# A two-layer trunk: attention scores in three f32r products, an earlier start of the second projection, the dense stage's loads in another order, and the mLSTM cell's state update and squares moved

## The chip, the cores and the metric

The kernel runs on one core of a Trainium2 chip. Its time is device microseconds (us) of one execution on that core. Engines are called by their names in the profile: PE is TensorE's matmuls, PEld its weight loads, DVE is VectorE, ACT is ScalarE, POOL is GpSimd and SP is SyncE, which here only issues DMAs. "SPq" and "ACTq" are these engines' queues of issued DMAs and waits. Each engine works through its own instructions in order; semaphores tie them together.

## The reference, cut to what matters

Two layers on a sequence of 2048 positions of width 1024. Layer 0 runs an S5 recurrence and an mLSTM cell side by side; layer 1 is sliding-window attention. All in fp32.

```
h = x
# layer 0
proj = rmsnorm_mod(h) @ ev_w_in;  s5_u, s5_z, m_in, m_z = split(proj)
y_s5 = s5(s5_u) * silu(s5_z)                      # chunked scan, then a gated product with w_glu
xc = silu(conv(m_in)); q, k = xc @ wq, xc @ wk; v, o = m_in @ wv, sigmoid(m_in @ wo)   # per head, 4 heads of 256
for each chunk of 128 positions, each head:       # the mLSTM cell
    s = (q k^T) * exp(gates);  num = s v + g * q C;  den = sum(s) + g * q n
    C = decay * C + (w_k * k)^T v;  n = decay * n + sum(w_k * k)
    h_cell = num / max(|den|, exp(-m))
y_m = (rmsnorm(o * h_cell) * norm_g + skip * xc) * silu(m_z)
h = h + gate0 * (concat(y_s5, y_m) @ ev_w_out)
# layer 1
q, k, v, z = split(rmsnorm_mod(h) @ od_w_in);  q, k = rope(rmsnorm(q)), rope(rmsnorm(k))
for each block of 128 queries, window of 256 keys, 16 heads of 64, 4 key heads:
    p = softmax(masked(q k^T / 8), with a sink);  a = p v
h = h + gate1 * ((a * silu(z)) @ od_w_out)
```

## The kernel before

The program is a row of stages with a barrier between them: `startup`, `front` (first half of the first projection), `project2` (second half of it, with the S5 recurrence beside it), `glu`, `dense`, `cell`, `attend_in`, `attend`. Large products are made from values split into an f32r part and its f32r rest: ScalarE rounds (a CAST), VectorE subtracts, and TensorE adds three products (high by high, high by rest, rest by high), each of 128x128 weights and 512 columns.

**`project2` (L914).** For 64 groups g, `state(g)` makes two products of the group's matrices (L1207, L1208, out of a ring of buffers `s_wt` that SyncE fills), `gemm(s)` is a unit of 24 matmuls of the projection, and `y(g)` the group's output. TensorE's order is `state(s)`, `gemm(s)`, `y(s−1)`.

**`dense` (L1555).** 16 units u: for head u // 4 and 512 positions, the products for q and k (from `x`, i.e. `xc`, the first 12 matmuls) and for v and o (from `m`), and beside them the output product of the S5 half. `unit(u)` is on SyncE the load of both inputs (L1617, L1618 into `bridge`), on ScalarE their rounding (L1720, L1723), on VectorE the rests (L1786). `head(h)` loads and splits a head's weights into `e_wh`. `result(u, j)` on ScalarE takes one result out of PSUM and stores it. `gates` are the cell's gates, made from logits in small steps between the units; `Gates.transfers(sp, part)` (L1456) is SyncE's share: part 0 stores the logits, part 2 waits for VectorE's chunk ends and stores them (L1469).

**`cell` (L1916).** 16 chunks c of 128 positions, each with four heads h. Chunk c's instructions on each engine:
- TensorE, `first(c, h)`: transpose of the keys and scores (`xp_ks`, L2391, L2393), then queries by state (`xp_bb`, L2402). `second(c, h)`: keys by values (`xp_c`, C0 and C1, L2414, L2415), then scores by values (`xp_aa`, L2419). It goes `first(c, h+1)` before `second(c, h)`. The output product of the chunk before (`xp_o`, L2442 to L2444, 24 matmuls for each half n) and the transposes of `x_hs` (L2430) stand between the heads.
- ScalarE: `first(c, h)` scales keys (`x_kw`, L2092) and `BB` (`x_bs`, L2096); `square(c, h)` (L2100); `exps(c)` (L2080) makes the decays `x_pm` of chunk c, at the end of chunk c−1; `y_part` (L2123) rounds the output; `norm(c)` (L2135) squares the finished residual row of chunk c and sums it, for the next layer's norm.
- VectorE: `weigh(c, h)` (`x_st`, L2197) scores by decays; `state(c, h)` (L2203, L2204) adds C0 and C1 to the state `x_c`; `output(c, h)` (L2212 to L2222); `blend` (L2244, L2251); `residual(c, n)` (L2262) adds the output product to the residual.
- GpSimd: for each chunk one mask step (L2073) out of `gate_run`, input of `exps`.
- SyncE, in this order in each turn, all on one queue: `store(c−1)` (L2019), `residual(c)` (L2015), `xc(c+1)` (L2002), `inputs(c+2)` (keys L1988, queries L1989, `gate_run` L1992, values L1996, L1997), `z(c+1)` (L2007). This turn takes place while the engines work on chunk c+1.

The residual row has two buffers, so its load waits for the square of the chunk two before:

```python
def residual(c):
    if c >= 2:
        sp.wait_ge(h_out[c % 2], 16 * (c // 2))
        sp.wait_ge(h_squared, c - 1)
```

**`attend_in` (L2514).** 40 units of 24 matmuls: the projection into q, k, v, z. q and k are turned by VectorE (`rope`) into a ring `rst` of two, and SyncE stores each piece to `q_d`, `k_d`.

**`attend` (L3025).** 64 steps G (16 blocks t, 4 key heads g). In step G TensorE makes the products of weights by values of an earlier step (`b_pv`, L3251), the scores (`b_psc`, L3228) in fp32 on 64 rows, two heads side by side, the transposes of exponentials (`b_t`, L3238) and 12 matmuls of the output product (`b_po`, L3266 to L3268). The rest of a step goes over ScalarE (L3124), GpSimd (L3113) and VectorE (L3167).

## Time and profile before

| | |
|---|---|
| median of 3 runs | 2952.21 us (2948.35 to 2953.49) |
| the profiled execution | 2948.46 us, span 2946.6 us |
| PE busy | 2750.8 us, 93% of the span |
| PEld, DVE, ACT, POOL busy | 2184.4, 1584.6, 1099.7, 642.4 us |
| mean granted clock of TensorE | 0.969 |

By the first and last instructions of the stages: `project2` about 493 to 1042, `dense` 1210 to 1590, `cell` 1590 to 2047, `attend_in` 2047 to 2546, `attend` 2550 to 2946. A timeline gives the start of an instruction in us, its length, engine and line, the operation with its output and input, how many instructions the row stands for, and in brackets the idle time of the engine before it with what ended it. The waits are a table of engine and line, what ended the wait, us in total, number, longest.

### The profile page before, as it was taken

The page shows a single profiled execution, that of the slowest core. Times are in us where ns is not written, and L with a number is a line of the kernel's source. Part 1 is how long each engine was busy: PE and PEld are TensorE (multiplying, and loading weights), DVE is VectorE, ACT ScalarE, POOL GpSimd, SP SyncE. Part 2 cuts the span into 40 slices and gives each one's busy share as a digit, 9 for nine tenths or more (in the row PEclk, how much of TensorE's full clock was granted, in tenths as well). Part 3 has the DMA queues.
Part 4 walks back from the last instruction along what each step waited for, and adds up shares of the span by engine and source line. Part 5 has one row for each costly group of instructions (what it writes and reads, how often), then busy time and mean ns, then how long its engine had stood idle before and what let it go on. Part 6 is the DMA issues. An engine that isn't in the chain of part 4 may idle for free. (4 is left out here: it accounts for less than half of the span.)

```text
span 2946.6 us, 36815 instructions
## 1 busy us (share of the span) xinstructions
PE 2750.8 (93%) x13147; PEld 2184.4 (74%) x13147; DVE 1584.6 (54%) x3226; ACT 1099.7 (37%) x2380; POOL 642.4 (22%) x528
## 2 busy tenths in 40 slices
PE   4899998999999899799998799998999999899999
PEld 2787887888888678678886677776787777667776
DVE  5475771555665457454444666665533331466664
ACT  3612221222222223334432555554422221466664
POOL 0005651444545100022322000000000000133332
PEclk7999999999999899899998899998999999999999
DMA  8226446444554554788986565764322223522221
GB/s 278 88 70 149 152 152 146 142 148 143 147 154 149 164 202 165 256 252 247 292 269 203 146 171 163 211 166 136 99 70 80 77 84 117 164 65 86 87 92 60
DMA packets 461515, 445.07 MB, mean 151 GB/s; under 512 B 149685, under 2 KB 357901, under 8 KB 459917
## 3 DMA queue, kind: packets, MB, share of 16 engines
q1 hardware_dynamic: 357828, 337.20, 38.6%
q10 hardware_dynamic: 103504, 105.51, 10.7%
q8 instruction: 106, 1.74, 0.3%
q14 instruction: 77, 0.62, 0.1%
HBM read 280.98 MB, written 162.70 MB: 151 GB/s over the span
## 5 line engine op out<-in xcount | busy, mean ns | idle before, releaser
L2964 PE MATMUL a_pg<-a_hT,a_whl 128*128 128x512 f32 x640 | 256.8, 401 | 3.4 <-DVE a_whl L902 3.4
L2965 PE MATMUL a_pg<-a_hT,a_whl 128*128 128x512 f32 x640 | 251.2, 392 | 0.0
L2966 PE MATMUL a_pg<-a_hT,a_whl 128*128 128x512 f32 x640 | 250.9, 392 | 0.0
L908 PE MATMUL p_g<-hT,w_hl 128*128 128x512 f32 x512 | 212.3, 415 | 0.0
L854 PE MATMUL pg<-hT,w_hl 128*128 128x512 f32 x512 | 206.0, 402 | 6.4 <-DVE w_hl L902 6.4
L856 PE MATMUL pg<-hT,w_hl 128*128 128x512 f32 x512 | 201.5, 394 | 0.0
L855 PE MATMUL pg<-hT,w_hl 128*128 128x512 f32 x512 | 201.4, 393 | 0.0
L910 PE MATMUL p_g<-hT,w_hl 128*128 128x512 f32 x512 | 200.3, 391 | 0.0
L909 PE MATMUL p_g<-hT,w_hl 128*128 128x512 f32 x512 | 199.8, 390 | 0.0
L2964 PEld LDWEIGHTS a_pg<-a_hT,a_whl 128*128 128x128 f32 x640 | 121.4, 190 | 42.0 <-DVE a_whl L902 12.3
L2966 PEld LDWEIGHTS a_pg<-a_hT,a_whl 128*128 128x128 f32 x640 | 121.3, 190 | 26.3
L2965 PEld LDWEIGHTS a_pg<-a_hT,a_whl 128*128 128x128 f32 x640 | 121.6, 190 | 23.6
L1110 POOL TENSOR_TENSOR s_region<-s_wt 128x512 f32<-128x512 f32 x64 | 72.2, 1129 | 301.5 <-DMA s_wt<-s5w_d 301.3
L1130 DVE TENSOR_TENSOR s_region<-p_v,s_region 128x512 f32<-128x512 f32 x64 | 44.1, 690 | 166.0 <-PE p_v L1208 157.3
L3113 POOL TENSOR_TENSOR shared<-shared,b_stat 128x1024 f32<-128x1024 f32 x43 | 81.5, 1895 | 184.1 <-DVE b_stat L3180 184.1
L854 PEld LDWEIGHTS pg<-hT,w_hl 128*128 128x128 f32 x512 | 97.4, 190 | 29.4 <-DVE w_hl L902 7.3
L1395 PE MATMUL g_ps<-g_gh,g_w 128*128 128x512 f32 x256 | 101.5, 396 | 13.2 <-DVE g_gh L1297 10.0
L856 PEld LDWEIGHTS pg<-hT,w_hl 128*128 128x128 f32 x512 | 97.3, 190 | 21.0
L855 PEld LDWEIGHTS pg<-hT,w_hl 128*128 128x128 f32 x512 | 97.5, 190 | 19.1
L910 PEld LDWEIGHTS p_g<-hT,w_hl 128*128 128x128 f32 x512 | 96.2, 188 | 20.7
L909 PEld LDWEIGHTS p_g<-hT,w_hl 128*128 128x128 f32 x512 | 96.5, 188 | 20.0
L908 PEld LDWEIGHTS p_g<-hT,w_hl 128*128 128x128 f32 x512 | 96.6, 189 | 19.7
(546 smaller groups left out, 6854.2 us busy)
## 6 DMA issues: line engine op xcount, KB each, us to landing
s_wt<-s5w_d SPq DMA_DIRECT2D x64, 354.0 KB
w_raw<-in_ev_w_in SPq DMA_DIRECT2D x32, 512.0 KB, 6.1
s5w_d<-gate_sums SPq DMA_DIRECT2D x32, 512.0 KB, 3.1
vo_d<-e_stage ACTq DMA_DIRECT2D x64, 256.0 KB, 3.8
ada_w<-in_ada_w SPq DMA_DIRECT2D x32, 384.0 KB, 7.9
shared<-h_d SPq DMA_DIRECT2D x24, 512.0 KB, 3.9
a_raw<-in_od_w_in SPq DMA_DIRECT2D x38, 256.0 KB, 3.4
gate_sums<-h_d SPq DMA_DIRECT2D x18, 512.0 KB, 4.0
```

The lines of the kernel that those rows point to most:

```text
L854: nc.tensor.matmul(out, w[:, 0, k, :], x[:, 0, k, :], start=(k == 0), stop=False)
L855: nc.tensor.matmul(out, w[:, 0, k, :], x[:, 1, k, :], start=False, stop=False)
L856: last = nc.tensor.matmul(out, w[:, 1, k, :], x[:, 0, k, :], start=False, stop=(k == KC - 1))
L908: nc.tensor.matmul(out, w(0, k), x(0, k), start=(k == 0), stop=False)
L909: nc.tensor.matmul(out, w(0, k), x(1, k), start=False, stop=False)
L910: last = nc.tensor.matmul(out, w(1, k), x(0, k), start=False, stop=(k == n - 1))
L1110: table.add(nc.gpsimd.tensor_tensor(v4(pt), hi, lo(EBS), ALU.mult))
L1395: nc.tensor.matmul(ps[n][:], w(0), gh[:, 0, k, :], start=(k == 0), stop=False)
L2964: mm(bank, w[:, 0, k, :], x[:, 0, k, :], start=(k == 0), stop=False)
L2965: mm(bank, w[:, 0, k, :], x[:, 1, k, :], start=False, stop=False)
L2966: last = mm(bank, w[:, 1, k, :], x[:, 0, k, :], start=False, stop=(k == KC - 1))
L3113: nc.gpsimd.tensor_tensor(p, p, st[G % 3][:, 4].unsqueeze(2).broadcast_to([P, 4, 2 * P]), ALU.mult).then_inc(p_ready, 1)
```

## The change

- **`project2`**: in turn 0, TensorE does `gemm(0)` ahead of `state(0)`.
- **`dense`**: on SyncE the loads of unit 2 and of `y(1)` go ahead of the gates' first store and of the residual; heads 1 to 3 are loaded one unit later; `transfers(2)` goes from turn 2 to turn 3, behind unit 4's loads. On ScalarE and VectorE the rounding of `x` of unit 1 is separated from that of `m` and goes between results 4 and 5 of unit 0.
- **`cell`**: `state(c−1, 3)` goes ahead of `weigh(c, 0)` on VectorE, `blend(0)` ahead of a weight step; on ScalarE `norm(c−2)` at the end of turn c becomes `norm(c−3)` in the middle of it, behind `first(c, 2)`. SyncE's instructions are as they were.
- **`attend_in`**: each q piece is rounded (`q_round`) and its rest made (`q_rest`), and both are stored, to `q_d` and to a new `ql_d`; stores go out a unit later.
- **`attend`**: scores as three f32r products from `b_q_hi`, `b_q_lo`, `b_k_hi`, `b_k_lo`; the keys are split in five pieces, at the start and in steps 1, 9, 22, 38; the rests of the queries are loaded too. Some buffers get other places.

```diff
...
                 for s in range(LAST + 2):
-                    if s < LAST:
+                    if s == 0:
+                        gemm(0)
+                        state(0)
+                    elif s < LAST:
                         state(s)
                         gemm(s)
...
+        if part == "bias":
+            sp.dma_start(self.bias[:], self.a["m_b_if"].rearrange("o n -> n o"), allow_slow_non_contiguous=True).then_inc(self.bias_in, 16)
         if part == 0:
-            sp.dma_start(self.bias[:], self.a["m_b_if"].rearrange("o n -> n o"), allow_slow_non_contiguous=True).then_inc(self.bias_in, 16)
             sp.wait_ge(self.logits, 1)
             sp.dma_start(m.gt_d, m.gacc[:]).then_inc(self.moved, 16)
...
-                gates.transfers(sp, 0)
+                gates.transfers(sp, "bias")
                 for k in range(KC // 2, KC):
                     out_weight(k)
+                unit(2)
+                y(1)
                 sp.dma_start(gate[:], m.gate_d[0:1].broadcast_to([P, D])).then_inc(gate_in, 16)
                 x(0)
+                gates.transfers(sp, 0)
                 modulation(0)
                 for u in range(1, UNITS):
                     if u > 1:
                         modulation(u - 1)
-                    if u + 1 < UNITS:
-                        unit(u + 1)
-                    y(u)
-                    if u % NB == 1 and u // NB + 1 < MH:
+                    if u > 1:
+                        if u + 1 < UNITS:
+                            unit(u + 1)
+                        y(u)
+                    if u % NB == 2 and u // NB + 1 < MH:
                         head(u // NB + 1)
                     if u >= 2:
                         store(u - 2)
                     x(u)
-                    gates.transfers(sp, u)
                     if u == 2:
                         sp.wait_ge(wo_lo, KC)
+                    elif u == 3:
+                        gates.transfers(sp, 2)
+                    if u != 2:
+                        gates.transfers(sp, u)
...
-                def unit(u):
+                def unit_x(u):
                     act.wait_ge(*((x_in, 32 * u) if u else (m.ahead, 16 * 6)))
                     if u:
+                        act.wait_ge(g_done, 8 * u - 4)
+                    nc.scalar.copy(xhl[:, 0], x_raw).then_inc(u_hi, 1)
...
+                        if (u, j) == (0, 5):
+                            unit_x(1)
+                        if u == 0 and j % 2 == 1:
+                            out_weight(j // 2)
+                        if u == 1 and j >= 4:
+                            out_weight(j)
                         result(u, j)
...
-                        unit(u + 1)
+                        if u:
+                            unit_x(u + 1)
+                        unit_m(u + 1)
...
+                            if k == 2:
+                                unit_x(1)
                             out_weight(k)
+                    if u == 0:
+                        unit_m(1)
...
                     first(c, 2)
+                    if c >= 3:
+                        norm(c - 3)
                     if c >= 2:
                         y_part(c - 1)
+                    if c == LAST:
+                        norm(LAST - 2)
...
                         exps(c + 1)
                     square(c, 2)
-                    if c >= 2:
-                        norm(c - 2)
...
+                    if c:
+                        state(c - 1, MH - 1)
                     weigh(c, 0)
                     if c:
                         output(c - 1, MH - 1)
-                        state(c - 1, MH - 1)
                         variance(c - 1)
...
                     output(c, 2)
+                    if c == 1:
+                        blend(0)
                     weight_of(c, 3)
                     if c == 1:
-                        blend(0)
                         y_part(0)
...
+                        sp.wait_ge(q_rounded, i - KS_ + 1)
+                        sp.dma_start(place(m.q_d), q_hi[i % 2][:].bitcast(F32)).then_inc(r_out[i % 2], 16)
+                        sp.wait_ge(q_rested, i - KS_ + 1)
+                        sp.dma_start(place(m.ql_d), q_lo[i % 2][:].bitcast(F32)).then_inc(r_out[i % 2], 16)
...
-                    if u >= 2:
-                        store(*order[u - 2])
+                    if u >= 3:
+                        store(*order[u - 3])
...
+                def q_round(n, b):
+                    if KINDS[n] != "q":
+                        return
+                    i = rope_no[n, b]
+                    act.wait_ge(roped, i + 1)
+                    if i >= KS_ + 2:
+                        act.wait_ge(r_out[i % 2], stores(i))
+                    nc.scalar.copy(q_hi[i % 2][:], rst[i % 2]).then_inc(q_rounded, 1)
...
+                def q_rest(n, b):
+                    if KINDS[n] != "q":
+                        return
+                    i = rope_no[n, b]
+                    v.wait_ge(q_rounded, i - KS_ + 1)
+                    if i >= KS_ + 2:
+                        v.wait_ge(r_out[i % 2], stores(i))
+                    tt(q_lo[i % 2][:], rst[i % 2], q_hi[i % 2][:].bitcast(F32), ALU.subtract).then_inc(q_rested, 1)
...
+        pieces = (0, 2 * P, P + BT, P + 2 * BT, P + 3 * BT, P + 4 * BT)
+        SPLIT = {1: 1, 9: 2, 22: 3, 38: 4}
...
+                def q_rest(t):
+                    if t >= 2:
+                        sp.wait_ge(s_done, 4 * (t - 1))
+                    sp.dma_start(q_lo[t % 2][:].bitcast(F32), tiled(m.ql_d)[t]).then_inc(ql_in[t % 2], 16)
...
+                def k_hi(i):
+                    cols = slice(pieces[i], pieces[i + 1])
+                    nc.scalar.copy(khl[0][:, :, cols], kT[:, :, cols]).then_inc(k_rounded, 1)
+
+                k_hi(0)
                 for G in range(STEPS + 3):
+                    if G in SPLIT:
+                        k_hi(SPLIT[G])
...
+                def k_lo(i):
+                    v.wait_ge(k_rounded, i + 1)
+                    cols = slice(pieces[i], pieces[i + 1])
+                    tt(khl[1][:, :, cols], kT[:, :, cols], khl[0][:, :, cols].bitcast(F32), ALU.subtract).then_inc(k_split, 1)
+
+                k_lo(0)
...
                     for r in range(2):
-                        for h in range(2):
-                            rows = slice(AD * h, AD * (h + 1))
-                            last = mm(psc[:, 2 * h + r, :], qt[t % 3][rows, 4 * Q + 2 * x + r, :], kT[rows, Q, P * t:P * t + 2 * P],
-                                      start=True, stop=True)
+                        for e, (w, k) in enumerate(((q_hi[t % 3], khl[0]), (q_hi[t % 3], khl[1]), (q_lo[t % 2], khl[0]))):
+                            for h in range(2):
+                                rows = slice(AD * h, AD * (h + 1))
+                                last = mm(psc[:, 2 * h + r, :], w[rows, 4 * Q + 2 * x + r, :], k[rows, Q, P * t:P * t + 2 * P],
+                                          start=(e == 0), stop=(e == 2), skip_group_check=True)
...
```

ScalarE's instructions in one turn of the cell's loop, from the third head's `bs` on. In brackets stand reused semaphores by their first names: `p1_out0` is `h_squared`, which L2135 raises and waits for in its own order. Before, the square is the last of the turn, behind `exps` (L2080) and `square` (L2100):

```order
L2096 ACTIVATE x_bs0<-xp_bb,gate_cols 128x257 [waits n0_root_ready,s5_c_ready]
L2123 CAST x_yhl<-x_y 128x1024 [waits n_x_in1,p1_w_lo]
L2100 ACTIVATE x_ha,x_small0<-x_hs0 128x256 [waits s5_dve]
L2092 ACTIVATE x_kw1<-xp_ks1,gate_cols 128x256 [waits s5_angle_ready,s5_c_turned]
L2096 ACTIVATE x_bs1<-xp_bb,gate_cols 128x257 [waits n0_root_ready,s5_c_ready]
L2116 ACTIVATE x_xs<-x_xc,cols 128x128 [waits p1_w_lo,mod_w_in7]
L2116 ACTIVATE x_xs<-x_xc,cols 128x128 x7
L2080 ACT_TABLE_LOAD
L2080 ACTIVATE x_pm1<-x_pm1,gate_cols 128x128 [waits mod_gate_out]
L2080 ACTIVATE x_pm1<-x_pm1,gate_cols 128x128 x3
L2100 ACTIVATE x_ha,x_small0<-x_hs0 128x256 [waits s5_dve]
L2135 ACTIVATE gate_row0,n_stat<-gate_sums 128x1024 [waits p1_out0,p1_read]
```

The same stretch of ScalarE after, from the third head's `kw` on (the lines are numbered 27 higher; the square is L2162):

```order
L2119 ACTIVATE x_kw0<-xp_ks0,gate_cols 128x256 [waits s5_angle_ready,s5_c_turned]
L2123 ACTIVATE x_bs0<-xp_bb,gate_cols 128x257 [waits n0_root_ready,s5_c_ready]
L2162 ACTIVATE gate_row0,n_stat<-gate_sums 128x1024 [waits p1_out0,p1_read]
L2150 CAST x_yhl<-x_y 128x1024 [waits n_x_in1,p1_w_lo]
L2127 ACTIVATE x_ha,x_small1<-x_hs1 128x256 [waits s5_dve]
L2119 ACTIVATE x_kw1<-xp_ks1,gate_cols 128x256 [waits s5_angle_ready,s5_c_turned]
L2123 ACTIVATE x_bs1<-xp_bb,gate_cols 128x257 [waits n0_root_ready,s5_c_ready]
L2143 ACTIVATE x_xs<-x_xc,cols 128x128 [waits p1_w_lo,mod_w_in7]
L2143 ACTIVATE x_xs<-x_xc,cols 128x128 x7
L2107 ACT_TABLE_LOAD
```

The square has moved from behind `exps` to directly behind the third head's `bs`, ahead of the rounding of `y` (L2150). The queue that waits for it is SyncE's, of the changed kernel, where L2042 is the residual's load and L2019 that of `gate_run`:

```order
L2042 DMA gate_sums<-h_d 128x1024 [waits p1_out0,mod_w_in0]
L2029 DMA x_xc<-xc_d 128x8x128 [waits s5_c_in]
L2015 DMA x_k<-ck_d 128x8x128 [waits s5_c_ready,s5_c_turned]
L2016 DMA x_q<-cq_d 128x8x128
L2019 DMA gate_run<-gb_d 128x4x128 [waits mod_gate_out]
L2023 DMA x_vo<-vo_d 128x4x256 [waits s5_dve,s5_unit_ready]
L2024 DMA x_vo<-vo_d 128x4x256
```

This order is that of before. On VectorE, at the head of a chunk, the state update of the chunk before (L2203, L2204) stood behind the first `weigh` (L2197) and the five steps of `output`:

```order
L2262 TENSOR_TENSOR gate_sums<-gate_sums,xp_o0 128x512 [waits mod_gate_turned,n_x_in1]
L2197 TENSOR_TENSOR x_st0<-xp_ks0,x_pm0 128x128 [waits s5_a_in,s5_unit_ready,n_x_in2,s5_c_turned]
L2212 TENSOR_TENSOR x_ha<-xp_aa,x_bs1 128x257 [waits n_squared,n0_squared,s5_unit_ready]
L2215 SCALAR_TENSOR_TENSOR x_small1<-x_ha 128x1 [waits n0_root_ready]
L2216 TENSOR_TENSOR x_small1<-x_small1,gate_cols 128x1 [waits s5_in_mats]
L2217 RECIPROCAL x_small1<-x_small1 128x1 [waits s5_in_mats]
L2222 SCALAR_TENSOR_TENSOR x_hs1<-x_ha,x_small1,x_vo1 128x256 [waits s5_in_mats]
L2203 SCALAR_TENSOR_TENSOR x_c<-x_c,decay,xp_c0 128x257 [waits s5_angle_ready]
L2204 SCALAR_TENSOR_TENSOR x_c<-x_c,decay,xp_c1 128x257
```

The same place on VectorE after:

```order
L2291 TENSOR_TENSOR gate_sums<-gate_sums,xp_o0 128x512 [waits mod_gate_turned,n_x_in1]
L2232 SCALAR_TENSOR_TENSOR x_c<-x_c,decay,xp_c0 128x257 [waits s5_angle_ready]
L2233 SCALAR_TENSOR_TENSOR x_c<-x_c,decay,xp_c1 128x257
L2226 TENSOR_TENSOR x_st0<-xp_ks0,x_pm0 128x128 [waits s5_a_in,s5_unit_ready,n_x_in2,s5_c_turned]
L2241 TENSOR_TENSOR x_ha<-xp_aa,x_bs1 128x257 [waits n_squared,n0_squared,s5_unit_ready]
```

The update now stands first, ahead of the instruction that waits for `x_kw` and `x_pm`.

## Rows read from the trace of the kernel before

**Rows 1.** The page: busy time, share of the span and instructions of each engine.
```profile
PE 2750.8 (93%) x13147; PEld 2184.4 (74%) x13147; DVE 1584.6 (54%) x3226; ACT 1099.7 (37%) x2380; POOL 642.4 (22%) x528
```

**Rows 2.** The waits, of PE and SP: line, releaser: us, times, longest.
```profile
PE xp_c L2414 <- ACT x_kw L2092: 13.6, 12, 1.3
...
PE p_v L1207 <- DMA s_wt<-s5w_d: 7.8, 1, 7.8
...
SPq L1469 <- DVE t_ends L1522: 13.3, 1, 13.3
```

**Rows 3.** Timeline of PE in the dense stage, after its two stalls.
```profile
1232.88 0.79 PE L1865 MATMUL e_pg<-e_x,e_wh 128*128 128x512 f32 x1 [5.51 <-DVE e_x L1786]
...
1308.80 0.79 PE L1865 MATMUL e_pg<-e_x,e_wh 128*128 128x512 f32 x1 [6.72 <-DVE e_x L1786]
```

**Rows 4.** Stretches; us, then busy PE, PEld, DVE, ACT, POOL, PEclk, DMA share, GB/s.
```profile
501.50:504.00 2.50, 2.50 (x7) 1.95 (x7) 0.00 (x0) 0.00 (x0) 2.42 (x4) 0.50 1.10 270
1233.00:1238.00 5.00, 5.00 (x12) 3.94 (x13) 2.10 (x2) 0.63 (x2) 0.00 (x0) 0.50 0.93 343
...
1818.00:1821.00 3.00, 3.00 (x14) 2.52 (x15) 2.07 (x8) 1.72 (x3) 0.00 (x0) 1.00 1.15 315
1824.00:1827.00 3.00, 2.56 (x19) 2.13 (x18) 1.91 (x7) 0.00 (x0) 0.00 (x0) 1.00 0.24 40
2100.00:2500.00 400.00, 395.16 (x1758) 311.25 (x1757) 134.77 (x177) 101.92 (x147) 0.31 (x1) 0.99 0.29 87
```

**Rows 5.** Timeline of PE in the cell, head of chunk 8.
```profile
1815.56 1.14 PE L2402 MATMUL xp_bb<-x_c,four 128*128 128x257 f32 x4 [0.22 <-ACT x_bs L2096]
1817.90 0.67 PE L2414 MATMUL xp_c<-wide,x_kw 128*128 128x257 f32 x2 [1.20 <-ACT x_kw L2092]
...
1819.08 0.58 PE L2442 MATMUL xp_o<-x_wout,x_yhl 128*128 128x512 f32 x1
...
1826.38 0.38 PE L2391 MATMUL xp_ks<-ident,four 128*128 128x128 f32 x2
```

**Rows 6.** Timeline of DVE in the cell, same place.
```profile
1817.27 0.48 DVE L2204 SCALAR_TENSOR_TENSOR x_c<-x_c,decay,xp_c 128x257 f32<-128x257 f32 x1
```

**Rows 7.** Timeline of ACT in the cell, one period.
```profile
1812.07 1.28 ACT L2080 ACTIVATE x_pm<-x_pm,gate_cols 128x128 f32<-128x128 f32 x4
...
1813.65 1.04 ACT L2135 ACTIVATE gate_row<-gate_sums 128x1024 f32<-128x1024 f32 x1
...
1814.69 0.46 ACT L2092 ACTIVATE x_kw<-xp_ks,gate_cols 128x256 f32<-128x256 f32 x1
...
1827.25 0.47 ACT L2092 ACTIVATE x_kw<-xp_ks,gate_cols 128x256 f32<-128x256 f32 x1 [3.41 <-PE xp_ks L2393]
1828.12 0.48 ACT L2096 ACTIVATE x_bs<-xp_bb,gate_cols 128x257 f32<-128x257 f32 x1 [0.40 <-PE xp_bb L2402]
...
1838.43 1.28 ACT L2080 ACTIVATE x_pm<-x_pm,gate_cols 128x128 f32<-128x128 f32 x4
```

**Rows 8.** Timeline of SP and POOL in the cell, same period.
```profile
1814.86 0.33 SPq L2015 DMA_DIRECT2D gate_sums<-h_d  x1
...
1818.84 1.62 SPq L1992 DMA_DIRECT2D gate_run<-gb_d  x1
...
1829.72 1.26 POOL L2073 TENSOR_TENSOR x_pm<-causal,gate_run 128x512 f32<-128x512 f32 x1 [23.51 <-DMA gate_run<-gb_d]
```

**Rows 9.** DMA issues: KB each, median us from issue to landing.
```profile
gate_run<-gb_d SPq DMA_DIRECT2D x16, 256.0 KB, 11.3
```

**Rows 10.** Timeline of PE in the attention stage, one step.
```profile
2702.76 1.14 PE L3228 MATMUL b_psc<-keys,shared 64*128 64x256 f32 x8
2703.82 1.09 PE L3238 MATMUL b_t<-ident,shared 128*128 128x128 f32 x8
...
2704.99 0.39 PE L3267 MATMUL b_po<-wout,b_yhl 128*128 128x512 f32 x1
2705.22 0.40 PE L3268 MATMUL b_po<-wout,b_yhl 128*128 128x512 f32 x1
```

More of the change, by code:

```diff
@@ L1758, in result @@
                         act.dma_start(m.vo_d[NB * b + j - 4, :, h], s[:]).then_inc(st_out[g % 4], 16)
-                unit(0)
+                unit_x(0)
+                head(0, 0)
+                unit_m(0)
+                head(0, 1)
                 for u in range(UNITS):
@@ L1791, in head, with unit_x, unit_m @@
                     sub(wh[h % 2][:, 1, :, part], wh_raw[:, :, part], wh[h % 2][:, 0, :, part]).then_inc(wh_lo, 1)
[L1793 removed]
+                def unit_x(u):
                     v.wait_ge(u_hi, 2 * u + 1)
                     sub(xhl[:, 1], x_raw, xhl[:, 0]).then_inc(u_lo, 1)
[L1796 to L1797 removed]
+                def unit_m(u):
                     v.wait_ge(u_hi, 2 * u + 2)
                     sub(mhl[:, 1], m_raw, mhl[:, 0]).then_inc(u_lo, 1)
[L1800 to L1801 removed]
                 def y(t):
@@ L1832, in residual @@
                         tt(ht[t % 2][:, cols], ht[t % 2][:, cols], up[:, cols], ALU.add).then_inc(added, 1)
-                unit(0)
+                unit_x(0)
+                head(0, 0)
+                unit_m(0)
+                head(0, 1)
                 for u in range(UNITS):
@@ L1846, in _ @@
                         head(u // NB + 1, 1)
-                    if u + 1 < UNITS:
-                        unit(u + 1)
+                    if u and u + 1 < UNITS:
+                        unit_x(u + 1)
+                        unit_m(u + 1)
                     if u == 2:
@@ L2545, in attend_in @@
         pick = sb("a_pick", [P, 2, P])
+        q_hi = [nc.alloc_sbuf_tensor_at(f"a_q_hi{j}", [P, BT], F32R, offset=m.gate_at + 4 * j * BT) for j in range(2)]
+        q_lo = [nc.alloc_sbuf_tensor_at(f"a_q_lo{j}", [P, BT], F32R, offset=at) for j, at in enumerate((m.rq_at, m.rinv_at))]
+        q_no = {nb: i for nb, i in rope_no.items() if KINDS[nb[0]] == "q"}
+        KS_ = len(rope_no) - len(q_no)
+        stores = lambda i: 16 * ((min(i, KS_) + 1 - i % 2) // 2 if i < KS_ else KS_ // 2) + 32 * (max(i - KS_, 0) // 2)
         qa_pair = sb("a_qa", [P, 2 * BT])
@@ L2771, in _ @@
                     out(n, b)
+                    q_round(*order[u - 1])
                     v_turn(*order[u - 1])
@@ L2919, in _ @@
                     rope(*order[u - 1])
+                    q_rest(*order[u - 2])
                     if (n, b) == (ROPED[-1] + 1, 2):
@@ L2926, in _ @@
                         v.wait_ge(var_ready, 1)
-                        v.wait_ge(r_out[0], 16 * len(rope_no) // 2)
+                        for j in range(2):
+                            v.wait_ge(r_out[j], stores(len(rope_no) + j))
                         rsqrt_steps(nc, L, var, root, m.rinv[:], rst[0])
@@ L3057, in attend @@
         S = lambda names: (m.sem(f"b_{n}") for n in names.split())
+        ql_in = [m.sem(f"b_ql_in{j}") for j in range(2)]
         q_in, z_in, h_in, o_out = ([m.sem(f"b_{n}{j}") for j in range(3)] for n in ("q_in", "z_in", "h_in", "o_out"))
@@ L3344, in trunk @@
         at += (TT + 1) * AKV * AD
-        m.qt0, m.zt0 = (m.shared[:, at + j * D:at + (j + 1) * D].rearrange("p (i c) -> p i c", i=KC) for j in range(2))
+        m.q_hi0 = nc.alloc_sbuf_tensor_at("q_hi0", [P, KC, P], F32R, offset=m.shared_at + 4 * at)
+        m.q_lo0 = nc.alloc_sbuf_tensor_at("q_lo0", [P, KC, P], F32R, offset=m.spare_at)
+        _, m.zt0 = (m.shared[:, at + j * D:at + (j + 1) * D].rearrange("p (i c) -> p i c", i=KC) for j in range(2))
         m.shared_used = at + 2 * D
```

68 lines of the change are left out of this document (40 added, 28 removed).

## The prediction

> **What bounds the kernel now.** I read four views in this order. The page's busy times [rows 1]: TensorE is busy for 93% of the span, so the time is its work plus its waits and what its clock loses after them. The waits of TensorE [rows 2]: those this change aims at are 13.6 us in the cell, ahead of the products for the state (C0), and one of 7.8 us ahead of the second projection. The timelines [rows 3, 5 to 8] show the work around them. The stretches [rows 4] show the clock: after each of three idle times of 5.5, 6.7 and 7.8 us the granted clock stood at 0.50, TensorE's 1.2 GHz level, until about 11 us after the idleness began. The profiled execution took 2948.46 us, 3.7 us under the median of 2952.21, so I sum against 2948.5 and add 3.7.
>
> **Second projection's start.** Before, TensorE waits 7.8 us for the first cell matrices [rows 2]. After, the 24 matmuls of `gemm(0)`, which need nothing new, go ahead. At the pitch of two f32r matmuls of 512 columns, 0.23 us [rows 10], they are 5.45 us, all in place of waiting. The wait left is 2.3 us, short enough, I take, to leave the clock alone: around the cell's waits of 1.2 us it stays at 1.00, in the stretch from 1818 [rows 4]. The half clock after it [rows 4] covers some 3.3 us of work, of which half, 1.65, comes back. Sum −7 (from −5, if the clock falls all the same).
>
> **Dense stage.** Its first stall is 5.5 us long and ends at 1232.88 [rows 3]: ScalarE rounds unit 1's `x` only after all eight results of unit 0. After, that stands behind result 4, some 5 us earlier, and the subtraction behind the second output weight. TensorE would go on at about 1227.2. The 5.5 us go, and the half clock of the stretch from 1233 [rows 4] with them, 2.6 us; `m`, still rounded late, holds the second half back by about 0.6. That makes −7. The second stall, 6.7 us, ends at 1308.80 [rows 3]: SyncE stood 13.3 us in `transfers(2)` [rows 2] ahead of unit 4's loads. After, `transfers(2)` stands behind them, one unit later; 6.7 and 2.3 of clock go, −9. What pays: `gt_d`'s store and the heads' weights go out later, but the weights still land some 10 us ahead of need. I take −15 for both (−18 to −5, the low end if another load is next to be late).
>
> **The cell, state update first.** One chunk period is 26.36 us, the distance of the two `exps` rows [rows 7]. Call K the start of `kw(c, 0)` on ScalarE, 1814.69 here. TensorE starts `C0(c, 0)` at K+3.21 [rows 5], since `state(c−1, 3)`, whose second instruction starts at 1817.27 [rows 6], stood on VectorE behind `weigh(c, 0)` and four more. With the state update first, C0 follows the `BB` group, which starts at K+0.87 and takes 0.87 (the same distance as `kw(c, 2)` to `bs(c, 2)`, 1827.25 to 1828.12 [rows 7]): K+1.74, a gain of 1.47 per chunk. `blend(0)` ahead of `weight_of` gives about 1.2 once.
>
> **The cell, squares moved: the term that decides.** `norm` is the square with a sum over a row of the residual (L2135, at 1813.65 [rows 7], 1.04 us to the next instruction's start). Before, `norm(c−3)` closes iteration c−1. The change puts it into the middle of iteration c, behind `first(c, 2)`. But SyncE waits for exactly this square before it loads `residual(c−1)` into the same buffer, and on SyncE's in-order queue everything for the next chunk stands behind: `xc(c)`, keys and queries of c+1, then `gate_run`. GpSimd's mask needs `gate_run`, and `exps(c+1)` at the end of the same iteration c needs the mask. Before, the residual load goes at 1814.86, `gate_run` at 1818.84, GpSimd starts at 1829.72 and `exps` at 1838.43 [rows 7, 8]: 14.9 us from the residual load to GpSimd, and 7.4 us of slack after GpSimd's 1.26. After, the residual load comes some 12 us later in the period than now (K+0.17 against K+13.5 below), and a closed chain sets the period. From K:
> C0(c, 0) at 1.74; C0, C1 and AA 1.18 (1817.90 to 1819.08); outputs, turn and residual additions 7.30 (1819.08 to 1826.38) [rows 5]; scores to `kw(c, 2)` 0.87 (1826.38 to 1827.25) and to `bs(c, 2)` another 0.87, itself 0.36 till the next can start; the square and SyncE's answer 1.21 (1813.65 to 1814.86) [rows 7, 8]: the residual load at K+13.5. The rounding of `y` behind the square starts some 0.6 later; its matmuls stand behind those of two more heads and don't feel it. Then 14.9 to `gate_run`'s arrival, or 15.3 with the median landing of 11.3 in place of 10.9 [rows 9], GpSimd 1.3, and from `exps` to the next `kw` 1.58 (as 1812.07 to 1814.69 [rows 7] less the removed square, 1.04). Sum 31.3 to 31.7, take 31.5.
> TensorE then idles 6 to 7 us in every chunk, which is the length that brought the half clock in all three cases above and cost 1.65, 2.3 and 2.7. The slowed stretch is the head of the chain (scores, C0, C1, outputs), so its 2.2 us are on the path: period 33.7. That is 7.35 more than now, for the twelve periods from chunk 3 to 15: +88. The other chunks gain 1.47 each and the 1.2: −6. Cell +82. Bounds: without a clock loss 31.3, twelve times 4.9 is +59, less 6, +53; with a loss of 3 and 1.5 more for landing and mask, 36.0, +109. Could the arrival be sooner, since the loads now start in a calmer stretch? While `gate_run` is on its way the DMA engines run at a share of 0.24 and 40 GB/s, in the stretch from 1824 [rows 4]; its 10.9 us are its own (each row goes to 128 partitions), not a queue's. So I keep 14.9 to 15.3.
> The Trainium skill ("DMA: Bandwidth & Descriptors", section "Bandwidth") gives 6.15 us for 1 MB, at 341 GB/s. By that the 2.25 MB up to and with `gate_run` would take 6.9 us, and the cell would pay nothing; the row of 14.9 us speaks against it.
>
> **Attention's input stage.** 32 roundings on ScalarE (0.6 us), 32 subtractions on VectorE (0.7 us) and 32 more stores of 256 KB, beside a TensorE that is busy for 395 of 400 us while ScalarE is for 102 and VectorE for 135, in the stretch from 2100 [rows 4]. Covered: 0. Without cover, ScalarE stopping for stores behind a weight load, up to +5.
>
> **Attention.** Before, four pairs of fp32 matmuls on 64 rows take 1.06 us of TensorE's time, from `b_psc` to `b_t` [rows 10]. After, there are six pairs in f32r; at half the 512-column pitch of 0.23, 0.115, they take 0.69. Of the 1.06 some 0.2 is the change of group, which stays, so 0.17 is saved (0.37 if it doesn't stay). In some 56 of 64 steps TensorE is the bound: −10 (−21 to −8). Added: the keys' first split before the first score, +1.4, and four more inside steps whose ScalarE and VectorE have some 0.4 us to spare, 0.7 each, +3. Net −6.
> The Trainium skill ("TensorE: Matmul & The Clock Gate", Part 3, "The mechanism") says that a weight load overlaps matmuls in flight only where the row groups differ; the f32r matmuls of 128 rows in [rows 10] keep 0.23 with loads between them, so here I don't follow it.
>
> **Sum.** 2948.5 − 7 − 15 + 82 + 0 − 6 = 3002.5, with 3.7 to the median 3006.
>
> **Rivals.**
> A, faster: the late square costs nothing. This decides at the time from residual load to arrival: the chain closes within 26.36 if it is at most 26.4 − 13.5 − 1.3 − 1.6 = 10.0 us. Then the cell gains 15 × 1.47 + 1.2 = 23, and the time is 2948.5 − 7 − 15 − 23 − 6 + 3.7 = 2901. For it: the queues are calmer in that stretch. Against: 14.9 measured, of which `gate_run` alone, once issued, 10.9. Chance 0.07. The figure of the Trainium skill ("DMA: Bandwidth & Descriptors", section "Bandwidth") cited above would give this case.
> B: the chain closes, but the clock stays full, or falls only where TensorE isn't on the path. Period 31.5, +61 − 6 = +55, time 2979. For it: between stalls TensorE works 25 us at full load; against: three of three such waits lost the clock. 0.20.
> C: the chain is heavier, landing and mask 1.5 us slower or the clock loss 3 us. Period 36.0, +109, time 3033. 0.13.
> D: the f32r pairs in attention don't go at half pitch. If a pair of half-height matmuls costs 0.215 whatever its type (the 1.06 less 0.2, over four), six cost 1.29, +0.43 in 56 steps, +24 in place of −10: 3040 on top of the forecast. 0.04.
> E: the gains in front and the cell's loss cancel within 0.2%, or a move doesn't do what it says: 0.03, near 2950.
>
> **How the numbers follow.** The forecast case (period 33.7) has 0.53. The range from 2970 to 3038 holds it, B and most of C. A and E are outside below, a part of C and D above: about 0.17 left out. Faster by over 0.2% (about what a measurement of this kernel can tell from no change) is A and a part of E: 0.08. Within 0.2%: 0.02. Slower: 0.90.
>
> **Signs in the profile after.** Distance of the cell's `kw(c, 0)` rows: 26.4 becomes 31 to 36; 25 would be A. SyncE's wait for the square at the residual load grows, TensorE's idle time in the cell ends on ScalarE and through it on GpSimd and `gate_run`, and the clock there shows 0.50 stretches. GpSimd's start of the mask lies some 28 us behind K. C0(c, 0) starts 1.7 behind K, or more at half clock. The 7.8 us wait becomes 2.3; the two waits of `e_pg` for `e_x` vanish. `b_psc` to `b_t` goes from 1.06 to 0.9. Most of this is wrong if `gate_run` lands within 10 us of the residual load, or if SyncE's queue stands otherwise than written.

## The result and the profile after

The changed kernel takes 3037.28 us in the median of four runs (3035.72 to 3045.81), the kernel before beside it 2952.85. The ratio is 1.0294, with an interval of 95% from 1.0279 to 1.031: 87 us slower. The forecast was slower by 54, at 3006 us, and it named the cell's late square as the cause. The direction and the cell's mechanism held; the size was 33 us short, of which 15 are the dense stage's, whose forecast gain didn't come, and 10 the cell's. And the ratio on the median of before that stood ahead of the prediction gives 3039, just over the range's end of 3038.

Where the time went, by the first or last matmul of each stage in the two profiled executions (us from the start of the span; the stage's own change in the last two columns):

| up to | before | after | change of the stage | as forecast |
|---|---|---|---|---|
| end of the second projection (`p_gate`) | 1010.2 | 1006.0 | −4 | −7 |
| start of `dense` | 1214.8 | 1211.8 | +1 | 0 |
| end of `dense` (`e_pg`) | 1584.7 | 1581.7 | 0 | −15 |
| end of the cell (`xp_o`) | 2044.8 | 2134.2 | +92 | +82 |
| end of attention's input stage (`a_pg`) | 2546.1 | 2637.8 | +2 | 0 |
| end of attention (`b_po`) | 2942.5 | 3029.7 | −4.5 | −6 |

One or two us in a row of this table are no effect by themselves: attention's input stage takes from 501.3 to 503.7 us in the traces of this study, and 501.3 both in the kernel before and in the one with attention's part of the change alone.

The page's busy times of the changed kernel answer to [rows 1]:

```profile
PE 2776.3 (92%) x13403; PEld 2213.7 (73%) x13403; DVE 1609.0 (53%) x3263; ACT 1116.5 (37%) x2417; POOL 640.0 (21%) x528
```

TensorE's busy time grew by 26 us only (it has 256 matmuls more, and more of them at half clock); the rest of the 87 is waiting. The waits, PE's and SP's, answer to [rows 2]:

```profile
PE xp_bb L2433 <- ACT x_bs L2123: 79.9, 15, 7.0
...
PE e_pg L1892 <- DVE e_x L1807: 9.2, 3, 8.2
...
SPq L2039 <- ACT gate_row L2162: 242.7, 13, 24.0
```

The 13.6 us ahead of C0 and the 7.8 us of the second projection have gone. In their place stand 3.6 us at the second projection's start (below) and one large new wait of 79.9 us, in the cell, of `BB(c, 1)` for ScalarE's scaling of the head before. ScalarE is only its last link. One period of the cell shows the others: ScalarE first, then SyncE and GpSimd, then TensorE, in the changed kernel (they answer to [rows 5, 7, 8]):

```profile
1880.15 1.28 ACT L2107 ACTIVATE x_pm<-x_pm,gate_cols 128x128 f32<-128x128 f32 x4 [7.04 <-POOL x_pm L2100]
...
1881.73 0.45 ACT L2119 ACTIVATE x_kw<-xp_ks,gate_cols 128x256 f32<-128x256 f32 x1
...
1895.22 0.47 ACT L2119 ACTIVATE x_kw<-xp_ks,gate_cols 128x256 f32<-128x256 f32 x1 [3.91 <-PE xp_ks L2424]
...
1896.46 1.05 ACT L2162 ACTIVATE gate_row<-gate_sums 128x1024 f32<-128x1024 f32 x1
...
1914.64 1.28 ACT L2107 ACTIVATE x_pm<-x_pm,gate_cols 128x128 f32<-128x128 f32 x4 [7.26 <-POOL x_pm L2100]
...
1916.22 0.45 ACT L2119 ACTIVATE x_kw<-xp_ks,gate_cols 128x256 f32<-128x256 f32 x1
```

```profile
1897.69 0.33 SPq L2042 DMA_DIRECT2D gate_sums<-h_d  x1
...
1901.81 1.66 SPq L2019 DMA_DIRECT2D gate_run<-gb_d  x1
...
1913.35 1.26 POOL L2100 TENSOR_TENSOR x_pm<-causal,gate_run 128x512 f32<-128x512 f32 x1 [33.23 <-DMA gate_run<-gb_d]
```

```profile
1882.60 2.08 PE L2433 MATMUL xp_bb<-x_c,x_q 128*128 128x257 f32 x4 [6.04 <-ACT x_bs L2123]
```

Read it as a circle, K being `kw(c, 0)` at 1881.73: the square starts at K+14.7, SyncE's residual load follows at K+15.96, GpSimd's mask at K+31.6 (15.7 later), `exps` at K+32.9 and the next K at K+34.5. ScalarE waits 7.3 us for GpSimd, TensorE 6.0 us for ScalarE. Two stretches of the changed kernel show the clock, columns as in [rows 4]:

```profile
1880.00:1884.00 4.00, 1.40 (x3) 1.17 (x4) 1.59 (x6) 2.40 (x8) 0.12 (x1) 0.57 0.80 268
1884.00:1888.00 4.00, 4.00 (x12) 3.13 (x11) 1.96 (x8) 2.73 (x6) 0.00 (x0) 0.57 0.02 4
```

After the 6.0 us the granted clock of these stretches is 0.57, mostly the level of 1.2 GHz, as in the three cases of before.

### The profile page after: what moved, and what is told of

It is laid out like the page before. It is cut to its first block and busy times, and to the rows that moved or that the text cites. A ratio compares the mean times of both kernels' runs of the same rounds, so it can differ in the third digit from the quotient of the medians.

```text
span 3033.8 us, 37521 instructions
## 1 busy us (share of the span) xinstructions
PE 2776.3 (92%) x13403; PEld 2213.7 (73%) x13403; DVE 1609.0 (53%) x3263; ACT 1116.5 (37%) x2417; POOL 640.0 (21%) x528
## 5 line engine op out<-in xcount | busy, mean ns | idle before, releaser
L3031 PEld LDWEIGHTS a_pg<-a_hT,a_whl 128*128 128x128 f32 x640 | 121.9, 191 | 42.1 <-issue 12.8
L2100 POOL TENSOR_TENSOR x_pm<-causal,gate_run 128x512 f32<-128x512 f32 x15 | 19.7, 1313 | 470.7 <-DMA gate_run<-gb_d 470.7
L1399 PE MATMUL g_ps<-g_gh,g_w 128*128 128x512 f32 x256 | 101.6, 397 | 14.6 <-DVE g_gh L1301 10.4
L909 PEld LDWEIGHTS p_g<-hT,w_hl 128*128 128x128 f32 x512 | 96.7, 189 | 23.7 <-issue 4.0
L911 PEld LDWEIGHTS p_g<-hT,w_hl 128*128 128x128 f32 x512 | 96.5, 189 | 20.8
```

Source lines behind the costliest of these rows:

```text
L909: nc.tensor.matmul(out, w(0, k), x(0, k), start=(k == 0), stop=False)
L911: last = nc.tensor.matmul(out, w(1, k), x(0, k), start=False, stop=(k == n - 1))
L1399: nc.tensor.matmul(ps[n][:], w(0), gh[:, 0, k, :], start=(k == 0), stop=False)
L3031: mm(bank, w[:, 0, k, :], x[:, 0, k, :], start=(k == 0), stop=False)
```

## The experiments

Three theories stood against each other for the cell. Q, the prediction's: the late square holds SyncE's queue, so the decays' input comes late. V: VectorE's new order costs it. S: the square costs it by itself, in the middle of ScalarE's turn. Times below are medians; since the kernel before has medians from 2949.8 to 2952.9 us beside the different runs, the ratio beside each is what counts.

### The square put back

```diff
-                    if c >= 3:
-                        norm(c - 3)
...
-                    if c == LAST:
-                        norm(LAST - 2)
...
                     square(c, 2)
+                    if c >= 2:
+                        norm(c - 2)
```

> The changed kernel with the square of the residual row put back to the end of ScalarE's turn; all else as changed. Theory Q (the late square holds SyncE's queue, so the decays' input arrives late): the cell's period falls from 34.0 to about 24.9 us (26.4 of before less the 1.5 of the earlier state update), time about 3037 - 12 x 9.1 = 2928 us, between 2920 and 2936. Rival V (VectorE's new order, state update ahead of weighing, is what costs): nothing changes, 3037 us. SyncE's wait for the square goes back from 24 us at the longest to about 11.

Measured 2924.45 us, ratio 0.9917 (0.99 to 0.9933). From its first matmul to its last the cell takes 430 us in place of 542 (and of 450 before), and SyncE's longest wait for the square is 10.4 us (11.4 before). All of the loss, and more, came with the square; V falls.

### The late square alone

```diff
                     first(c, 2)
+                    if c >= 3:
+                        norm(c - 3)
...
                     square(c, 2)
-                    if c >= 2:
-                        norm(c - 2)
```

> The kernel before with one edit: the square moved into the middle of ScalarE's turn. Theory Q: the same closed chain, C0 1.5 us later than in the changed kernel, so a period of 34 to 36 us, +91 to +115 us on 2953: 3044 to 3068 us. Rival V: the kernel loses nothing or about a us, 2953.

Measured 3051.07 us, ratio 1.0341 (1.0324 to 1.0358): +101 us from the one moved square. The period from chunk 4 to 14 is 34.8 us, in the changed kernel 34.15. The difference is less than the 1.5 us by which C0 starts sooner in the changed kernel, but it has its sign.

### The late square, with the inputs ahead of it in SyncE's queue

```diff
-                    if c:
-                        residual(c)
                     if c + 1 < NMC:
                         xc(c + 1)
                     if c + 2 < NMC:
                         inputs(c + 2)
+                    if c:
+                        residual(c)
```

> The changed kernel, the square still late, but SyncE issues the next chunk's inputs (xc, keys, queries, gate_run, values) ahead of the residual row that waits for the square. Theory Q: gate_run no longer stands behind the square, period about 25 us, time 2925 to 2936 us, the same as with the square put back. Rival S (the square itself, in the middle of ScalarE's turn, delays scaling and rounding that TensorE waits for): the time stays near 3037; a mixture would show the 1.1 us of the square per chunk, +13 us over 2928.

Measured 2920.71 us, ratio 0.9903 (0.9885 to 0.9921). The square is where the change put it, and nothing is left of the loss: S falls too, and Q is shown from both sides. It's 116 us from the order of the residual load and the other loads. SyncE and GpSimd of this kernel:

```profile
1895.97 1.58 SPq L2019 DMA_DIRECT2D gate_run<-gb_d  x1
...
1911.36 0.34 SPq L2042 DMA_DIRECT2D gate_sums<-h_d  x1
```

```profile
1906.82 1.27 POOL L2100 TENSOR_TENSOR x_pm<-causal,gate_run 128x512 f32<-128x512 f32 x1 [23.82 <-DMA gate_run<-gb_d]
```

`gate_run` still needs 10.9 us from issue to GpSimd's start, but it is issued 15 us ahead of the residual row instead of 4 us behind it. That the residual row comes late hurts nobody: it is needed at the chunk's end only.

### `gate_run` directly behind the residual row

Three loads, `xc`, keys and queries, 1.5 MB together (the expectation's 2 MB counts the residual row too), stood between the residual row and `gate_run`. Here they follow it.

```diff
-                    if c >= 2:
-                        sp.wait_ge(masked, c - 1)
-                    sp.dma_start(gb, m.gb_d.rearrange("(h c) t -> c h t", h=MH)[c].partition_broadcast(P)).then_inc(gb_in, 16)
...
+                def decays(c):
+                    if c >= 2:
+                        sp.wait_ge(masked, c - 1)
+                    sp.dma_start(gb, m.gb_d.rearrange("(h c) t -> c h t", h=MH)[c].partition_broadcast(P)).then_inc(gb_in, 16)
...
                     if c:
                         residual(c)
+                    if c + 2 < NMC:
+                        decays(c + 2)
```

> The changed kernel, the square late and the residual load still first in SyncE's queue, but gate_run is issued directly behind it, ahead of xc, keys and queries (2 MB less in front of it). Theory Q with a landing that is gate_run's own (10.9 us measured from its issue): from the residual load to GpSimd 11.3 in place of 15.3 us, period 34.0 - 4 = 30, time about 2990 us (2980 to 3000). Rival L (the landing is that of the queue in front of it): it lands within some 5 us, the chain opens, period 25, time 2930 us.

Measured 3029.26 us, ratio 1.0272 (1.0255 to 1.0288): by the ratios 7 us better than the changed kernel, not 47, and not 107. Both expectations missed the time, and the traces say why. `gate_run` now lands 9.5 us in the median after its issue, against 11.3 behind the three loads, and GpSimd starts 10.1 us behind the residual load in place of 15.7. So most of the landing is `gate_run`'s own, as the prediction took it. But what stands behind it in the same queue then comes late. TensorE, the loads and a stretch of this kernel:

```profile
1941.42 0.69 PE L2427 MATMUL xp_ks<-ident,x_k 128*128 128x128 f32 x2 [6.37 <-DMA x_q<-cq_d]
```

```profile
x_k<-ck_d SPq DMA_DIRECT2D x8, 512.0 KB, 11.5
...
x_q<-cq_d SPq DMA_DIRECT2D x8, 512.0 KB, 12.8
```

```profile
1930.00:1934.00 4.00, 4.00 (x19) 3.22 (x18) 2.38 (x8) 0.99 (x4) 0.00 (x0) 1.00 0.25 48
```

The queries land 12.8 us after their issue where they took 7.7 in the changed kernel, and TensorE waits 6.4 us per chunk for them. The keys take 11.5 us in place of 6.5 and `xc` 10.7 in place of 5.2: all three loads behind `gate_run` are about 5 us later, while from 1930 to 1934 the DMA engines are busy for a share of 0.25 only. It is the whole group of loads behind the late residual row that is late, 2.25 MB with the broadcast; which of them the engines wait for is only a matter of their order. This stretch of the changed kernel has the same group on its way:

```profile
1899.00:1905.00 6.00, 5.47 (x25) 4.20 (x24) 4.48 (x14) 2.61 (x9) 0.00 (x0) 1.00 1.02 296
```

The Trainium skill ("DMA: Bandwidth & Descriptors", section "Bandwidth") gives 341 GB/s for transfers of 1 MB, measured there with GpSimd issuing them. The changed kernel moved 296 GB/s from 1899 to 1905, near that figure; `gate_run` alone, 256 KB in 9.5 us, is far below either.

### Work for the idle TensorE

Is it the idle time that slows the head of the chain? This kernel does more: in chunks 4 to 15, 40 needless transposes where TensorE waits.

```diff
+                    for _ in range(20 if h == 1 and c >= 4 else 0):
+                        for e in range(2):
+                            nc.tensor.transpose(KS[h % 2][:, e * P:(e + 1) * P], kt[j][:, 2 * h + e, :], m.ident[:])
```

> The changed kernel, square late, with 40 idle transposes more per chunk on TensorE (the transposes of the second head's keys, made 21 times, chunks 4 to 15), put where TensorE waits 5 to 7 us for the decays; each 0.11 us, 4.4 us of added work per chunk that nothing waits for. Theory G (the period is the closed chain, and its first part runs at half clock because TensorE idled): the clock stays at 1.00 there, the period falls from 34.0 to about 32, 3037 - 24 = 3013 us. Rival B (the clock's fall costs nothing, or the added work comes onto the path): 3037 us or more.

Measured 3016.26 us, ratio 1.0226 (1.0204 to 1.0248): 21 us less than the changed kernel, with 480 matmuls more. TensorE and a stretch of the kernel with the added work:

```profile
1868.78 4.53 PE L2423 MATMUL xp_ks<-ident,x_k 128*128 128x128 f32 x40
...
1875.26 0.92 PE L2436 MATMUL xp_bb<-x_c,x_q 128*128 128x257 f32 x3 [1.28 <-ACT x_bs L2123]
```

```profile
1876.00:1880.00 4.00, 4.00 (x19) 3.34 (x18) 3.00 (x11) 2.73 (x6) 0.00 (x0) 1.00 0.06 22
```

Here the clock stays at 1.00, and from `kw(c, 0)` to `kw(c, 2)` it is 11.1 us (1843.04 to 1854.16) in place of 13.5 (1881.73 to 1895.22). That is so in six of the eleven chunks from 4 to 14. In the other five the clock falls all the same and the distance is 12.8 us; the one from 1907 is such a chunk:

```profile
1908.03 1.14 PE L2436 MATMUL xp_bb<-x_c,four 128*128 128x257 f32 x4 [2.80 <-ACT x_bs L2123]
```

```profile
1910.00:1913.00 3.00, 3.00 (x9) 2.34 (x8) 2.61 (x10) 2.22 (x5) 0.00 (x0) 0.52 0.99 313
```

The waits left at this place are 1.9 to 2.8 us in the five and 1.2 to 2.5 us in the six, so their length alone doesn't say which it will be. The same distance has a mean of 13.3 us in these chunks of the changed kernel, so the half clock cost 2.2 us per period on the path, and the cause was idleness, as the forecast's term of 2.2 had it.

### The state update alone

```diff
+                    if c:
+                        state(c - 1, MH - 1)
                     weigh(c, 0)
                     if c:
                         output(c - 1, MH - 1)
-                        state(c - 1, MH - 1)
                         variance(c - 1)
```

> The kernel before with one edit: VectorE's state update of the last head ahead of the weighing. By the step of the prediction, C0 starts 1.5 us earlier in each of 15 chunks: 2952.5 - 22 = 2930 us. Rival P (the square, at its old place ahead of the first kw, keeps most of it): 1.5 less 1.0 per chunk, 2945 us.

Measured 2930.36 us, ratio 0.994 (0.9925 to 0.9955), 13 to 22 us less; the cell of its trace is 426.7 us long, 23 less than before. The step of the prediction (1.47 in each of 15 chunks) holds; the square ahead of the first `kw` takes nothing of it.

### The dense part alone

> The kernel before with the dense part of the change alone. By the prediction -15 us: 2936. By the trace of the changed kernel, in which both old stalls are gone and a new one of 8.2 us and one of 3.4 stand in their place: 2950 us, within 3.

Its edit is the whole of the diff's `dense` part and `Gates.transfers`. Measured 2953.19 us, ratio 0.9997 (0.9988 to 1.0007): nothing. Both old stalls are gone in the changed kernel's trace, but a new one of 8.2 us stands at 1278.85 and one of 3.4 us, for VectorE's gated output, at 1295.42 (8.0 and 3.3 us in the trace of this run). The larger one's row, then VectorE's and SyncE's ahead of it:

```profile
1278.85 0.79 PE L1892 MATMUL e_pg<-e_x,e_wh 128*128 128x512 f32 x1 [8.20 <-DVE e_x L1807]
```

```profile
1275.30 2.36 DVE L1807 TENSOR_TENSOR e_wh<-wide,e_wh 128x1024 fp32r<-128x1024 f32 x2 [11.22 <-ACT e_wh L1726]
1277.58 1.22 DVE L1807 TENSOR_TENSOR e_x<-bridge,e_x 128x1024 fp32r<-128x1024 f32 x1
```

```profile
1259.65 1.12 SPq L1646 DMA_DIRECT2D ada_w<-in_ada_w  x2
1260.82 0.59 SPq L1622 DMA_DIRECT2D bridge<-xc_d  x1
...
1264.50 0.47 SPq L1617 DMA_DIRECT2D wide<-in_m_wo  x1
```

VectorE splits head 1's weights ahead of unit 3's `x`, a unit before any matmul needs them. They were loaded at 1238 before and are loaded at 1263 now, so the split waits until 1274.16 on ScalarE. Unit 3's inputs, issued from 1260.82, took at most 8.5 us to land, so they were there by 1270; they wait behind the split. And SyncE itself comes to unit 3 at 1260.82 only, behind a wait of 8.4 us for GpSimd to free the modulation weights' buffer.

### The heads' load back, and then the unit ahead of the modulation

```diff
-                    if u % NB == 2 and u // NB + 1 < MH:
+                    if u % NB == 1 and u // NB + 1 < MH:
                         head(u // NB + 1)
```

> The changed kernel with the next chunk's inputs ahead of the residual row on SyncE (2920.7 us measured for that alone), and in the dense stage heads 1 to 3 loaded in the turn of before. Theory H (the new dense stall of 8.2 us at 1270 to 1279 comes from head 1's weights, loaded a unit later, whose splitting stands on ScalarE and VectorE in front of unit 3's): the stall goes, with its half clock of some 2 us, 2909 to 2912 us. Rival U (unit 3's own inputs are late, behind SyncE's 8.4 us wait for GpSimd): the stall shrinks by less than 2 us, 2919 to 2921 us.

Measured 2916.48 us, ratio 0.9892 (0.9877 to 0.9906). The stage is 4.5 us shorter than in the kernel without this edit (2920.71 us, above), where 9 to 12 were expected. The stall is down from 8.0 to 3.48 us:

```profile
1273.59 0.79 PE L1892 MATMUL e_pg<-e_x,e_wh 128*128 128x512 f32 x1 [3.48 <-DVE e_x L1807]
```

H and U each hold a part: 4.5 us were the heads' weights, the rest comes with unit 3's own inputs: their loads are late (ScalarE waits 5.5 us for them), and VectorE's subtraction takes 2.17 us in place of 1.22. On top of this edit, the loads of the unit were then put ahead of the modulation's:

```diff
                     if u > 1:
-                        modulation(u - 1)
-                    if u > 1:
                         if u + 1 < UNITS:
                             unit(u + 1)
                         y(u)
+                        modulation(u - 1)
```

> The kernel of the last dense experiment (next chunk's inputs ahead of the residual row in the cell, heads loaded in the turn of before; 2916.5 us), and in each turn of the dense stage the next unit's loads on SyncE ahead of the modulation weights, whose load waits for GpSimd (8.4 us at 1259). Theory U (the 3.5 us left of the new dense stall are unit 3's inputs behind that wait): the stall goes with what its clock costs, about 1, 2911 to 2913 us. Rival W (the inputs can't go earlier, since the buffers come free only then, or the loads collide with head 1's weights): 2916 us.

Measured 2922.78 us, ratio 0.9901 (0.9884 to 0.9918), no gain: the stage is 5.0 us longer than with the edit before. Unit 3's stall is gone, but two others stand in its place. TensorE of this kernel:

```profile
1366.18 0.46 PE L1556 MATMUL e_pt<-ident,t_q 64*128 64x64 f32 x4 [1.90 <-ACT t_q L1548]
1370.81 0.79 PE L1891 MATMUL e_pg<-e_x,e_wh 128*128 128x512 f32 x1 [4.17 <-DVE e_x L1806]
```

One is of 4.1 us at 1285, for VectorE's gated output, the other of 1.9 and 4.2 us around the gates' turn at 1366. In both places VectorE is slow beside GpSimd:

```profile
1273.92 3.55 DVE L1514 TENSOR_TENSOR t_w<-t_w 64x128 f32<-64x128 f32 x1
...
1366.31 4.44 DVE L1806 TENSOR_TENSOR e_x<-bridge,e_x 128x1024 fp32r<-128x1024 f32 x1
```

```profile
1273.82 3.51 POOL L1713 TENSOR_TENSOR ada_sum<-ada_sum,ada_w 128x1536 f32<-128x1536 f32 x1
...
1365.38 4.29 POOL L1713 TENSOR_TENSOR ada_sum<-ada_sum,ada_w 128x1536 f32<-128x1536 f32 x1
```

In the changed kernel these two steps of VectorE take 0.28 and 1.22 us. The first and a step ahead of it, which takes 2.20 us, are 5.2 us longer than usual together, and VectorE goes on from them without a pause to the gated output; the second ends where the wait of 4.2 us ends. So the trace puts both stalls down to them in the main; no run moved GpSimd's instructions away to show it.

### The second projection and attention, each alone

> The kernel before with the second projection's start alone. By the prediction -7 us; by the trace of the changed kernel, in which TensorE can't start before 497.3 whatever comes first, -4.6 us: 2946 us.

Its edit is the `project2` part of the diff. Measured 2949.26 us, ratio 0.9986 (0.9977 to 0.9995), −4. The first matmul of the stage, in the changed kernel:

```profile
497.26 0.47 PE L909 MATMUL p_g<-hT,w_hl 128*128 128x512 f32 x1 [3.61 <-PEq L576]
```

> The kernel before with the attention part of the change alone (q rounded and stored in two parts, scores as three f32r products). By the prediction -6 us. By the two traces: attention's input stage +2.3, the gap before the first score +2.7, then -7.2, together -2: 2950 us. Rival D (weight loads of the f32r pairs don't overlap): slower than before by over 20 us.

Its edit is the diff's `attend_in` and `attend` parts. Measured 2945.99 us, ratio 0.9987 (0.9976 to 0.9999), −4 with an interval down to nothing. The scores of one step in the changed kernel, which answer to [rows 10]:

```profile
2800.22 0.39 PE L3328 MATMUL b_psc<-b_k_hi,b_q_hi 64*128 64x256 f32 x2
2800.45 0.28 PE L3328 MATMUL b_psc<-b_k_lo,b_q_hi 64*128 64x256 f32 x2
2800.57 0.29 PE L3328 MATMUL b_psc<-b_k_hi,b_q_lo 64*128 64x256 f32 x2
2800.70 0.28 PE L3328 MATMUL b_psc<-b_k_hi,b_q_hi 64*128 64x256 f32 x2
2800.81 0.29 PE L3328 MATMUL b_psc<-b_k_lo,b_q_hi 64*128 64x256 f32 x2
2800.94 0.28 PE L3328 MATMUL b_psc<-b_k_hi,b_q_lo 64*128 64x256 f32 x2
2801.14 1.09 PE L3338 MATMUL b_t<-ident,gate_row 128*128 128x128 f32 x8
```

A pair takes 0.12 us, half of the 0.23 of 512 columns, so its weight loads are hidden, and from the scores to the transposes it is 0.92 us in place of 1.06. The Trainium skill ("TensorE: Matmul & The Clock Gate", Part 3, "The mechanism") says that a load overlaps matmuls in flight only where row groups differ. Each pair here uses the same two row groups as the one before it, and the loads cost nothing that shows, so the trace disagrees here again.

## Where the prediction was right, and which step failed

**The direction and the cause** were right. The chain was read from the code's waits and the rows of before, link by link, and the trace after has the same links. K to the residual load, forecast 13.5 and 2.2 of half clock, is 15.96; from there to GpSimd, forecast 14.9 to 15.3, is 15.66; GpSimd and `exps` 1.3 and 1.6 as said. The period of 33.7 came out at 34.0 over the twelve periods from chunk 3 to 15 (408.1 us in all; before 316.8), so the term of +88 is +91.

**The other chunks of the cell** were taken as a gain of 6 and gave a loss of 1, the step that was short by 7 us. Until chunk 3 only 1.5 us came; and behind the last K, where the prediction went on counting 1.47, the changed kernel needs 47.9 us against 45.3. TensorE comes out of a wait of 5.9 us at 2087 there, so it starts the tail at half clock. Where the rest of the 2.6 us goes isn't taken apart.

**The dense stage** is the step that failed: −15 forecast, 0 measured, outside its range of −18 to −5. Both stalls vanished as said, and two new ones, of 8.2 and 3.4 us, took their place. What failed is the sentence on what pays: "the weights still land some 10 us ahead of need". The need was taken at TensorE's first matmul with these weights. But ScalarE and VectorE split them a unit earlier, in front of the next unit's input, so a transfer that TensorE doesn't need yet holds what it does need. The run with the heads' load put back gives 4.5 us of the stage to that. What is left are stalls of 3.5 and 2.2 us. For the first the trace shows unit 3's load, late in SyncE's queue behind the wait for GpSimd's buffer, but the run that put the load ahead of that wait gained nothing, so how the rest of the 15 us divides stays open.

**The second projection**: −7 forecast, −4 measured. The 5.45 us of work were set against the whole wait of 7.8, but half of it, until 497.26, is the start of the stage itself, which no order of matmuls can use; the old wait hid it. The wait left was taken as 2.3 us, too short for the clock; it is 3.6, and the clock falls.

**Attention**: −6 forecast, −4.5 in the traces, −4 alone. The steps were mis-sized each in its own way: a step is 0.12 us shorter (5.85 to 5.73), not 0.17; the four later splits of the keys cost nothing that the steps show, not 3; the start costs 2.7, not 1.4. D, the rival of unhidden weight loads, is refuted.

**The rivals.** A would have been 2901 us; it needed the arrival within 10 us of the residual load, and it is 15.7. The kernel that meets its condition in another way, with the inputs ahead of the residual row, gives 2921. B, no clock loss, is refuted by the 0.57 and by the kernel with added work. C's 3033 is nearest to the measured time, but not for its reason: neither the landing nor the clock was heavier, other stages didn't pay back what they were to. E, gains and losses that cancel, didn't come.

## What to carry to other kernels

Before you move an instruction, look for who waits for it outside the engines you compare: a square of one us, moved by half a turn on an engine with idle time, cost 101 us, since a DMA queue that works in order stood behind it. Put the load that waits longest for its buffer last in its turn, not first; here that turned the change from +87 to −29 us, and with the heads' load back to −32 (ratio 0.9892), the fastest kernel of this study. When a load is made later, take as its need the first engine that handles it, and what stands behind that in the engine's order.

## What the runs showed of the hardware

TensorE's clock fell after an idle time of 3.6 us: until 497.26 the changed kernel's TensorE does nothing, and then this stretch follows, mostly at the level of 1.2 GHz:

```profile
498.00:501.00 3.00, 3.00 (x9) 2.28 (x8) 0.00 (x0) 0.00 (x0) 0.00 (x0) 0.53 0.63 168
```

In the kernel with added work it fell in five chunks after waits of 1.9 to 2.8 us, and in six it didn't, after 1.2 to 2.5. More matmuls can mean less time: 480 needless ones in the cell's waits took 21 us off.

Loads behind `gate_run`, which goes to 128 partitions, landed late: `xc`, keys and queries some 5 us later than without it ahead of them, while the DMA engines were busy for a share of 0.25 and moved 48 GB/s. Why it holds them up, no run shows.

VectorE's instructions in the dense stage sometimes took as long as a GpSimd instruction beside them had left. In the changed kernel VectorE's step below, on 64x128 elements, stood until 1259.71, and GpSimd's addition ran until 1259.63:

```profile
1256.29 3.42 DVE L116 TENSOR_SCALAR t_w<-t_w 64x128 f32<-64x128 f32 x1
```

```profile
1256.03 3.60 POOL L1714 TENSOR_TENSOR ada_sum<-ada_sum,ada_w 128x1536 f32<-128x1536 f32 x1
```

In the kernel with the heads' load back, where GpSimd was through before it, the same instruction took 0.22 us.
